# Expert routing decided inside the output projection's stage, and the place map by 16-bit products

## The reference

```python
g_logits = xf @ w_group + b_group            # 4 groups
g_idx = argmax(g_logits); g_w = softmax(g_logits)[g_idx]
e_logits = (xf @ w_router + b_router).reshape(T, 4, 8)[g_idx]     # 8 experts of that group
top_p, top_i = top_k(softmax(e_logits), 2); top_p = top_p / sum(top_p)
expert_id = g_idx * 8 + top_i; gate = g_w * top_p
acc = sum over the two experts: gate * ((silu(xf @ wg) * (xf @ wu)) @ wd)
```

## Time and profile before

| | us |
|---|---|
| median of three runs | 1356.83 |
| the profiled execution | 1354.09 |
| its span, first to last instruction | 1352.2 |
| PE busy | 1163.5 (86%) |
| VectorE (DVE) busy | 577.6 (43%) |
| ScalarE (ACT) busy | 497.2 (37%) |
| GpSimd (POOL) busy | 293.5 (22%) |

### The profile page before, as it was taken

One profiled execution on the slowest core, in us unless ns is written; L12 is line 12 of the kernel. 1 busy time (PEld: TensorE's weight loads), 2 busy tenths in 40 slices (PEclk: granted clock), 3 DMA queues, 4 the chain that ended last, 5 costly groups with the idle time before them and its releaser, 6 DMA issues. The chain is left out here.

```text
span 1352.2 us, 20920 instructions
## 1 busy us (share of the span) xinstructions
PE 1163.5 (86%) x7681; PEld 884.9 (65%) x7681; DVE 577.6 (43%) x1131; ACT 497.2 (37%) x926; POOL 293.5 (22%) x438
## 2 busy tenths in 40 slices
PE   5999999999678999997784999838999999999810
PEld 4999999999545667665564788624555555555500
DVE  4432114440146777774552544382333333333336
ACT  4421221121136666765542322103444444444412
POOL 1101210122123334573000111101222222222124
PEclk9999999999779999999987999958999999999955
DMA  5302231121320000002845421177998999999255
GB/s 180 116 32 74 72 96 33 60 70 61 116 93 9 9 9 9 17 9 71 308 138 156 133 106 44 37 279 256 334 323 316 335 347 322 323 322 345 89 190 214
DMA packets 76154, 204.58 MB, mean 151 GB/s; under 512 B 13657, under 2 KB 34393, under 8 KB 67632
## 3 DMA queue, kind: packets, MB, share of 16 engines
q1 hardware_dynamic: 60416, 168.46, 35.9%
q0 software_dynamic: 15664, 35.09, 7.1%
HBM read 183.97 MB, written 37.09 MB: 163 GB/s over the span
## 5 line engine op out<-in xcount | busy, mean ns | idle before, releaser
L557 PE MATMUL psP<-w_hi,xn_hi 128*128 128x256 f32 (+1 forms) x864 | 249.0, 288 | 3.1 <-DVE xn_lo L442 2.0
L557 PE MATMUL psP<-w_lo,xn_hi 128*128 128x256 f32 (+1 forms) x864 | 243.4, 282 | 0.0
L557 PE MATMUL psP<-w_hi,xn_lo 128*128 128x256 f32 (+1 forms) x864 | 242.4, 281 | 0.0
L2152 PE MATMUL psG<-w_gu,xgT 128*128 (+1 forms) x528 | 239.6, 597 | 2.2 <-ACT xgT L2188 2.2
L2152 PEld LDWEIGHTS psG<-w_gu,xgT 128*128 128x128 f32 x528 | 98.2, 191 | 101.9 <-issue 96.6
L557 PEld LDWEIGHTS psP<-w_hi,xn_hi 128*128 128x128 f32 (+1 forms) x864 | 157.2, 182 | 4.2 <-DVE xn_lo L442 2.4
L557 PEld LDWEIGHTS psP<-w_lo,xn_hi 128*128 128x128 f32 (+1 forms) x864 | 157.3, 182 | 0.0
L557 PEld LDWEIGHTS psP<-w_hi,xn_lo 128*128 128x128 f32 (+1 forms) x864 | 157.0, 182 | 0.0
L2248 DVE TENSOR_TENSOR down_lo<-w_dn,down_hi 128x1024 fp32r<-128x1024 f32 x66 | 77.9, 1222 | 166.7 <-ACT down_hi L2196 166.7
L353 ACT ACTIVATE nat<-psP 128x256 f32<-128x256 f32 (+1 forms) x104 | 39.9, 383 | 233.9 <-PE psP L557 233.9
L969 DVE TENSOR_TENSOR_SCAN E<-E,edge 128x257 f32<-128x257 f32 (+7 forms) x32 | 81.8, 2556 | 19.2 <-POOL E L713 19.2
(11 more groups left out here) (309 smaller groups left out, 2015.0 us busy)
## 6 DMA issues: line engine op xcount, KB each, us to landing
w_gu<-in_w_gate SPq DMA_DIRECT2D x33, 1024.0 KB, 6.4
w_gu<-in_w_up SPq DMA_DIRECT2D x33, 1024.0 KB, 7.1
w_dn<-in_w_down SPq DMA_DIRECT2D x33, 1024.0 KB, 7.7
w<-in_w_in SPq DMA_DIRECT2D x18, 512.0 KB, 3.6
y<-expert_rows SPq DMA_DIRECT2D x16, 512.0 KB, 5.9
Kc<-in_cache_sb_k SPq DMA_DIRECT2D x4, 1024.0 KB, 6.2
Vc<-in_cache_sb_v SPq DMA_DIRECT2D x8, 512.0 KB, 7.0
Kc<-in_cache_diff_k SPq DMA_DIRECT2D x4, 1024.0 KB, 10.7
```

The costliest lines, as they stand in the source:

```text
L557: last = nc.tensor.matmul(psP[0:m, u % NPS, 0:BW], x[:, c, tok], y[b % 2][:, c, :], start=first, stop=final)
L2152: last = nc.tensor.matmul(psG[:, :].rearrange("p (o g f) -> p o g f", o=1, g=2), xgT[:, c, :], gu5[:, ds(slot, 1), :, c, :], start=(c == 0 ...
```

## The change

The decisions for a tile move from `route` into `mix_out`, as a function `decide(t0, t1)` on VectorE's list. It is called for tiles 0 to 2 at the end of round 3, for tiles 3 to 5 at the end of round 6, for tile 6 in round 8 ahead of the residual, and for tiles 7 and 8 behind the loop. Ms becomes bfloat16 with the tile index innermost. The two count products and the map's products take bfloat16 operands: a token number is split into a multiple of 16 and a rest, each exact in bfloat16, so that there are 36 products in place of 18. VectorE makes the 18 one-hots of rows in three instructions rather than 18, and GpSimd the products with the rests (`in_lo`). The chain from counts to places is rewritten with fewer instructions, the constants of it are set by GpSimd, and the gates are computed behind the map. ScalarE's two exponentials have no wait, and it loads the next activation table in `route`.

```diff
-    c["before"] = (q < k).astype(np.float32)
+    c["after"] = (q < k).astype(np.float32) - 1
...
-    c["pair"] = np.concatenate([(token + 1) * valid, (token + 1 + NTOK) * valid], 1).astype(np.float32)
+    pair = np.concatenate([(token + 1) * valid, (token + 1 + NTOK) * valid], 1)
+    c["pair_hi"] = (16 * np.floor(pair / 16)).astype(np.float32)
+    c["pair_lo"] = (pair % 16).astype(np.float32)
...
+        g["dve_own"], g["dve_count"] = sem(keep, "dve_own"), [0]
...
+        for n, shape, dt in (("gm", [P, NT, 8], F32), ("gf", [P, NT], F32), ("ge", [P, NT, NG], F32),
+                             ("dd", [P, NT], F32), ("ef", [P, NT, 2], F32), ("M", [P, 2, NT, NE], F32),
+                             ("Ms", [P, NE, NT], BF16), ("after_b", [P, P], BF16), ("ones_b", [P, P], BF16)):
+            g[n] = sb(keep, n, shape, dt)
...
         then(nc.gpsimd.memset(nh[:, :], -0.5))
+        nc.gpsimd.tensor_copy(g["after_b"][:, :], g["after"])
+        nc.gpsimd.tensor_copy(g["ones_b"][:, :], g["ones"])
...
+        def decide(t0, t1):
+            V, R = nc.vector, slice(t0, t1)
+            n = t1 - t0
...
+            GL = g["logits"][:, R, 0:NG]
+            EL = g["logits"][:, :, NG:].rearrange("p t (g e) -> p t e g", g=NG)
+            dve.wait_ge(r_kept, t1)
+            then(V.tensor_copy(gpad[:, R, 0:NG], GL))
+            for t in range(t0, t1):
+                last = V.max(gm[:, t, :], gpad[:, t, :])
+            then(last)
+            for t in range(t0, t1):
+                last = V.max_index(gi[:, t, :], gm[:, t, :], gpad[:, t, :])
+            then(last)
+            V.tensor_tensor(g["ge"][:, R, :], GL, gm[:, R, 0:1].to_broadcast([P, n, NG]), ALU.subtract)
+            then(V.tensor_copy(gf[:, R], gi[:, R, 0]))
+            then(V.tensor_tensor(oh[:, R, :], gf[:, R].unsqueeze(2).to_broadcast([P, n, NG]),
+                                 g["iota"][:, 0:NG].unsqueeze(1).to_broadcast([P, n, NG]), ALU.is_equal))
+            for t in range(t0, t1):
+                last = V.tensor_tensor(pr[:, t - t0, :, :], EL[:, t, :, :],
+                                       oh[:, t, :].unsqueeze(1).to_broadcast([P, EPG, NG]), ALU.mult)
+            then(last)
+            then(V.reduce_sum(sel[:, R, :], pr[:, 0:n, :, :], AX_X))
+            for t in range(t0, t1):
+                last = V.max(em[:, t, :], sel[:, t, :])
+            then(last)
+            for t in range(t0, t1):
+                last = V.max_index(ei[:, t, :], em[:, t, :], sel[:, t, :])
+            then(last)
+            V.tensor_tensor(g["dd"][:, R], em[:, R, 1], em[:, R, 0], ALU.subtract)
+            then(V.tensor_copy(ef[:, R, :], ei[:, R, 0:2]))
+            for x in range(2):
+                last = V.scalar_tensor_tensor(ef[:, R, x], gf[:, R], float(EPG), ef[:, R, x], ALU.mult, ALU.add)
+            then(last)
+            for x in range(2):
+                last = V.tensor_tensor(M[:, x, R], ef[:, R, x].unsqueeze(2).to_broadcast([P, n, NE]),
+                                       g["iota"][:, 0:NE].unsqueeze(1).to_broadcast([P, n, NE]), ALU.is_equal)
+            then(last)
+            last = V.tensor_tensor(Ms[:, :, R].rearrange("p e t -> p t e"), M[:, 0, R], M[:, 1, R], ALU.add)
+            if t1 == NT:
+                then(last)
+                V.tensor_tensor(Ms[:, :, FULL], Ms[:, :, FULL], g["valid"][:, FULL:].to_broadcast([P, NE]), ALU.mult)
+        nc.vector.memset(gpad[:, :, :], -3e38)
         then(nc.vector.memset(g["logits"][:, :, :], 0.0))
...
                 keep_T(("x", t - 1))
             if t + 2 < NT:
                 sub(t + 2)
+            if t == FULL:
+                decide(6, 7)
             if t < NT:
                 residual(t)
                 normalise(t)
             if t >= 1:
                 keep_logits(t - 1)
+            if t in (3, 6):
+                decide(t - 3, t)
+        decide(7, NT)
...
+    PART = 6
+    in_row = sb(st, "in_row", [P, 2 * NT, P], BF16)
+    in_tile = sb(st, "in_tile", [P, 2 * NT, MAPT], BF16)
+    in_hi = sb(st, "in_hi", [P, 2 * NT, MAPT], BF16)
+    in_lo = sb(st, "in_lo", [P, 2 * NT, MAPT], BF16)
...
     def _(pool):
-        nc.gpsimd.memset(g["xg"][:, :], 0.0).then_inc(zeroed, 1)
-        pool.wait_ge(zeroed, 1)
+        nc.gpsimd.memset(carry[:, :, :], 1.0).then_inc(set_up, 1)
+        pool.wait_ge(set_up, 1)
+        nc.gpsimd.memset(carry[:, :, 0:1], 0.0)
+        nc.gpsimd.memset(more[:, 0:1], float((NE - 1) * P)).then_inc(set_up, 1)
+        nc.gpsimd.tensor_scalar(base[:, :], g["iota"][0:1, 0:NE], 1.0, float(2 - NE), ALU.mult, ALU.add) \
+            .then_inc(set_up, 1)
+        nc.gpsimd.memset(g["xg"][:, :], 0.0).then_inc(set_up, 1)
+        pool.wait_ge(in_tile_ready, 1)
+        nc.gpsimd.tensor_tensor(in_lo[:, :, :], in_tile[:, :, :],
+                                g["pair_lo"].unsqueeze(2).to_broadcast([P, 2 * NT, MAPT]), ALU.mult).then_inc(lo_ready, 1)
+        pool.wait_ge(set_up, 4)
         pool.wait_ge(map_ready, 1)
         gather_tile(pool, nc, g, 0)
...
         V = nc.vector
-        GL = g["logits"][:, :, 0:NG]
...
-        then(V.memset(carry[:, :, :], 1.0))
-        then(V.memset(carry[:, :, 0:1], 0.0))
+        M, ef = g["M"], g["ef"]
+        dve.wait_ge(set_up, 2)
         dve.wait_ge(counts_full, 1)
-        then(V.tensor_copy(tot[:, :, :], psB[:, 0:NT * NE].rearrange("p (t e) -> p e t", e=NE)))
         then(V.tensor_tensor_scan(upto[:, :, :].rearrange("p e t -> p (e t)"),
-                                  carry[:, :, :].rearrange("p e t -> p (e t)"),
-                                  tot[:, :, :].rearrange("p e t -> p (e t)"), 0.0, ALU.mult, ALU.add))
-        V.tensor_copy(cnt[:, :], upto[:, :, NT - 1])
...
+                                  carry[:, :, :].rearrange("p e t -> p (e t)"), psB[:, 0:NT * NE], 0.0,
+                                  ALU.mult, ALU.add))
+        V.tensor_scalar(cnt_i[:, :], upto[:, :, NT - 1], -1.0, 0.0, ALU.add, ALU.max)
+        then(V.tensor_tensor(pos[:, :, :], upto[:, :, :], psA[:, 0:NT * NE].rearrange("p (e t) -> p e t", e=NE),
+                             ALU.add))
+        then(V.tensor_scalar(cnt_i[:, :], cnt_i[:, :], -P, None, ALU.bitwise_and))
+        then(V.tensor_scalar(more[:, 1:], cnt_i[:, :], float(-P), None, ALU.add))
+        then(V.tensor_tensor_scan(shift[:, :], more[:, :], more[:, :], 0.0, ALU.add, ALU.max))
+        then(V.scalar_tensor_tensor(far[:, :, :], pos[:, :, :], float(P), bc(shift[:, 0:NE], [P, NE, NT], 2),
                                     ALU.is_ge, ALU.mult))
         then(V.tensor_tensor(pos[:, :, :], pos[:, :, :], far[:, :, :], ALU.add))
...
+        V.tensor_scalar(tile_i[:, :], slot_i[:, :, :].rearrange(flat), 7, None, ALU.logical_shift_right)
+        then(V.tensor_scalar(row_i[:, :], slot_i[:, :, :].rearrange(flat), P - 1, None, ALU.bitwise_and))
+        V.tensor_tensor(in_tile[:, :, :], bc(tile_i[:, :], [P, 2 * NT, MAPT], 2),
+                        bc(g["iota"][:, 0:MAPT], [P, 2 * NT, MAPT], 1), ALU.is_equal).then_inc(in_tile_ready, 1)
+        V.tensor_tensor(in_row[:, 0:PART, :], bc(row_i[:, 0:PART], [P, PART, P], 2),
+                        bc(g["iota"], [P, PART, P], 1), ALU.is_equal).then_inc(rows_ready, 1)
+        dve.wait_ge(in_tile_ready, 1)
+        V.tensor_tensor(in_hi[:, :, :], in_tile[:, :, :], bc(g["pair_hi"], [P, 2 * NT, MAPT], 2), ALU.mult) \
+            .then_inc(hi_ready, 1)
+        for n in range(PART, 2 * NT, PART):
+            V.tensor_tensor(in_row[:, n:n + PART, :], bc(row_i[:, n:n + PART], [P, PART, P], 2),
+                            bc(g["iota"], [P, PART, P], 1), ALU.is_equal).then_inc(rows_ready, 1)
...
+        dve.wait_ge(map_full, 1)
...
         V.tensor_tensor(g["slot_token"][:, :], number[:, :], empty[:, :], ALU.add).then_inc(map_ready, 1)
+        V.tensor_copy(g["slot_row"][:, :], number[:, :])
+        dve.wait_ge(weights_exp, 1)
+        then(V.reduce_sum(gw[:, :], g["ge"][:, :, :], AX_X))
+        then(V.reciprocal(gw[:, :], gw[:, :]))
+        then(V.tensor_scalar(ed[:, :], g["dd"][:, :], 1.0, None, ALU.add))
+        then(V.reciprocal(ed[:, :], ed[:, :]))
+        then(V.tensor_tensor(g["gates"][:, :, 0], ed[:, :], gw[:, :], ALU.mult))
+        V.tensor_tensor(g["gates"][:, :, 1], g["gates"][:, :, 0], g["dd"][:, :], ALU.mult)
     @blk.scalar
     def _(act):
...
+        nc.scalar.activation(g["ge"][:, :, :], g["ge"][:, :, :], ACT.Exp)
+        nc.scalar.activation(g["dd"][:, :], g["dd"][:, :], ACT.Exp).then_inc(weights_exp, 1)
+        nc.scalar.preload_act_table_set("sigmoid_and_others")
     @blk.tensor
     def _(pe):
...
+        flat = g["Ms"][:, :, :].rearrange("p e t -> p (e t)")
+        nc.tensor.matmul(psB[:, 0:NT * NE], g["ones_b"][:, :], flat, start=True, stop=True)
+        nc.tensor.matmul(psA[:, 0:NT * NE], g["after_b"][:, :], flat, start=True, stop=True).then_inc(counts_full, 1)
+        for half, ready in ((in_hi, hi_ready), (in_lo, lo_ready)):
+            pe.wait_ge(ready, 1)
```

(51 more changed lines are left out.)

48 lines of the change are left out of this document (17 added, 31 removed).

## The result

The changed kernel takes 1359.76 us (median of 16 runs), the kernel before beside it 1355.30 (16 runs): ratio 1.0046, with its interval [1.0024, 1.0067], so 3.3 to 9.1 us slower. In a later set of runs it was 1358.82 against 1354.10, ratio 1.0018 [0.9986, 1.0049], which can't be told from no change. The change removes some 11 us from the routing and puts some 15 us in front of it.

The account below looks back on a forecast made before the run. PE's pace bounds the output projection and experts; VectorE's list, then the first gather, bounds routing. Terms 4.1+7.1+3.0-11.2 = +3.0 us, from a base of 1355.4, forecast 1358.5 us; range 1350 to 1364.

Parts of the forecast that it names:

- Stalls: Output projection, rounds 4 and 7: PE stands still 4.05 and 3.1 us for `mT_lo` behind batches of three; +7.1 us.
- Clock: Output projection: PE's clock drops after each of two new idle stretches, 1.5 us each; +3.0 us, between 0 and 6.
- rival 2: Slower: each stall keeps PE at 1.2 GHz twice as long, map 1.3 us late; +7.3 us, 1362.7; chance 0.33.
- Tail: After the last logits: the two-tile batch runs on VectorE with nothing beside it; +4.1 us, between 3.8 and 4.6.
- Routing's start to the scan: Start of routing: bfloat16 count products and hand-over take 1.0 us, bounds 0.6 and 2.4, where float32 took 2.4.
- counts to `in_tile`: Routing: the shortened chain from counts to `in_tile` takes 5.5 us where it took 7.7.
- One-tile batch: Output projection, ahead of a residual: hidden in VectorE's 4.90 us of idle time, cost 0.
- GpSimd last: Routing: GpSimd's `in_lo` waits for VectorE's two-tile work and ends last, 11.4+2.2 = 13.6 us from the start.
- The last 18 products: Routing, map: PE's products with `in_lo` come last and take 3.1 us, bounds 2.0 and 4.6.
- Landing: End of routing: the first gather, sharing with the weights' transfers, takes 6.1 us to land, up to 7.1.
- rival 1: Weight loads hold the stage: SP's list opens the next stage, routing gains 14.0; +0.2 us, 1355.6; chance 0.13.
- The routing's -11.2: Routing, from its start to PE's start on gathered rows: 25.4 us in place of 36.6, -11.2 us.

Follow-up runs that it names:

- the second profile: The changed kernel itself, unaltered, run and profiled again in the later set: 1358.82 us, ratio 1.0018 to the kernel before.
- the first and the third row of the table above: First: changed kernel run again, batches of three, three experts' weights, 1358.82 us. Third: changed kernel with batches of two behind both psTm readings, three experts' weights, 1352.33 us.

## Why the prediction came out

The mechanism was right in the stage before the routing, and the forecast (1358.5) lies 1.3 us below the median. Its likeliest outcome, within 0.3%, was missed in the first set (0.46%) and met in the later one (0.18%). By its terms:

- **Stalls**, predicted 4.05 and 3.1: 4.19 and 3.16. The order of VectorE's list and the slack of the earlier trace rows gave them. (The bounds beside them work out at 6.1 and 8.3, not 6.0 and 8.2, which changes nothing.)
- **Clock**, predicted 3.0: 10.75-7.35 = 3.4 us. Two spells of 3.4 us (half clock from 806.1 to 809.5 and from 853.8 to 857.2) account for 3.2 of it: PE still stood for the first 0.4, and half of the rest is lost. It is 2.9 to 4.3 in the other profiles with batches of three, so rival 2's 6 did not come. But the size is partly luck: in three of the five profiles with these batches the spell at the first stall was twice as long, as rival 2 has it, and in two of those the second stall had none.
- **Tail**, predicted 4.1: 3.73. **Routing's start to the scan**, 1.0: 0.8; **counts to `in_tile`**, 5.5: 5.63.
- **One-tile batch**, predicted 0: hidden, with 1.75 us to spare.
- **GpSimd last**, predicted because of the earlier trace rows: wrong. GpSimd started at 896.39, ahead of VectorE's `in_hi`, which then took 2.54 us; GpSimd ended at 898.69 and VectorE at 899.63. The Trainium skill's rule in "SBUF — State Buffer", section "SBUF: two separate sides", weighed in the prediction, fits what is seen: `in_hi` ended 0.94 us behind GpSimd's product, and without that product it takes 1.07 us in all. The price went elsewhere than I had put it: 1.47 us on `in_hi`, where I had 1.1 on the last products, and the map came early all the same.
- **The last 18 products**, predicted 3.1 in bounds of 2.0 and 4.6: 0.93, below the lower bound, at a granted clock of 0.50. I took the old pace of 0.22 for a pass from products that VectorE fed; 0.05 is what one costs when all are ready. But PE didn't set the map's end then: psMap was full at 902.61, while VectorE, without a pause, worked on `te` and the steps behind it until 903.28, and the map was ready 1.6 us after psMap was full, not 1.0. VectorE's own list made it 15.35 us in place of 17.7, barely inside the range of 15 to 20.5.
- **Landing**, predicted 6.1: 8.0, and 6.3 in the second profile. I took the gathers among the experts' transfers for the first one; here nine 1 MB loads had the transfers' engines at a share of 0.90.
- **What ends the routing**: I expected the gather alone. In this profile it was SP's list, rival 1's resource: PE begins 1.06 us behind the landing and 0.4 behind SP's last issue. But that load went out later than elsewhere, 24.9 us after the start, where it was 20.4 to 22.0 in the other four profiles with three experts' loads. In those four PE's first weight load (PEld) waits for the gather's landing, as forecast. Two of them, the first and the third row of the table above:

```profile
922.74 1.57 PEld L2150 LDWEIGHTS psXe<-const,xg 128*128 128x128 f32 x8 [9.62 <-DMA xg<-normed_scratch,token_idx]
908.83 1.57 PEld L2150 LDWEIGHTS psXe<-const,xg 128*128 128x128 f32 x8 [11.02 <-DMA xg<-normed_scratch,token_idx]
```

The loads slow the gather as well (4.2 to 4.4 us with six ahead of it, 6.3 to 8.0 with nine). The routing's -11.2 came out as -10.8 because a map 2.35 us early met a landing 1.9 and an opening 0.8 us late. In the second profile the landing came near the forecast, and the routing to -13.3.

So the sum of +3.0 is near the +4.2 and +3.8 measured partly by luck: in the first profile errors of over 2 us in the routing cancel, in the second a routing 2.1 us better than forecast is made up by 1.3 more for the clock and 1.7 in the rest, which the prediction put at nothing.

## What to carry to other kernels

Work on an engine that is idle half of the time isn't free: what counts is what stands next on its list and who waits for that. The decisions of six tiles, in two batches, cost 10.7 us ahead of a reading that PE waits for; in three batches behind it they cost the stage nothing. When a path gets shorter, look at which transfers it now overlaps; and take a product's pace only from rows in which its operands were all ready, and not from rows in which another engine fed it piece by piece.

## What the runs showed that was not expected

- A stall of 3 to 4 us came with no slow clock, by 3.4 us of it, or by about 7, in the same code; and the attention to cached tokens from about 702 to 716 us ran for the most part at half clock in 8 of 12 profiles. The second goes with 4 to 16 us at the logits of tile 2, a part of the spread of over 20 us that hides small gains.
- Two products of two tensors, one each on GpSimd and VectorE, take 2.30 and 2.54 us side by side; one behind the other on VectorE they take 1.07 each.
